# Second half's state-space output moved beside the first half's delta stages, its projection into the expert stage; expert up rows stacked and summed in strips

## What is computed

```python
# end of the first block
y = rms_norm(y * silu(z_ssm), ssm_norm_g)                # (512, 2048)
y_ssm = y @ w_branch_ssm                                 # 2048 x 1024
merged = sigmoid(g_att) * y_att + sigmoid(g_ssm) * y_ssm
x = x + gate * (merged @ w_out)
# second block
h = modulate(rms_norm_2(x, norm1_gain), shift1, scale1)
qa, ka, va, qkv_b, z_b, b_raw, a_raw = split(h @ w_in)   # 512+512+512+1536+512+4+4 columns
x = x + gate1 * (concat(band_attention(qa, ka, va), delta_rule(qkv_b, z_b, b_raw, a_raw)) @ w_out)
h2 = modulate(rms_norm_2(x, norm2_gain), shift2, scale2)
# PEER: per token 8 heads x 16 experts out of 16384
u, vv = expert_down[experts], expert_up[experts]         # rows of 1024
act = gelu(einsum("thkd,td->thk", u, h2))
y = einsum("thk,thkd->td", gates * act, vv)
x = x + gate2 * y
```

## Time and profile before

| | |
|---|---|
| median of 3 runs | 2975.04 us |
| span of the profiled execution | 2961.7 us |
| TensorE busy | 2601.6 us (88%) |
| VectorE busy | 1694.0 us (57%) |
| GpSimd busy | 1163.5 us (39%) |
| ScalarE busy | 790.8 us (27%) |
| DMA, mean over the span | 239 GB/s |
| DMA, expert rows | 147456 packets, 536.94 MB |
| mean granted TensorE clock | 0.954 |

### The profile page before, as it was taken

The page is one execution under the profiler, slowest core; times in us unless marked ns, Lnnn a source line. Parts: engine busy times, 40 slices in busy tenths (PEclk is TensorE's granted clock), DMA queues, the critical chain, the costliest instruction groups (busy, mean ns, idle before and its releaser), DMA issues.

```text
span 2961.7 us, 25890 instructions
## 1 busy us (share of the span) xinstructions
PE 2601.6 (88%) x8302; PEld 1362.8 (46%) x8302; DVE 1694.0 (57%) x3696; ACT 790.8 (27%) x1604; POOL 1163.5 (39%) x1091
## 2 busy tenths in 40 slices
PE   7999899999979979988899899979887777777787
PEld 3444444445544436477775465546432222222232
DVE  2059814345521244274379998765777777777764
ACT  2022402148720022233234323221312221222121
POOL 0000000023300000000057777666777777777776
PEclk8999999999989999999899899989999899999999
DMA  7214112222323233322379989999999999999998
GB/s 310 75 57 171 58 66 79 85 65 69 96 85 119 108 114 118 127 83 75 114 259 355 349 304 379 383 364 343 370 407 405 398 407 404 407 397 409 408 404 351
DMA packets 185462, 709.00 MB, mean 239 GB/s; under 512 B 20416, under 2 KB 43344, under 8 KB 175216
## 3 DMA queue, kind: packets, MB, share of 16 engines
q0 software_dynamic: 147456, 536.94, 47.0%
q1 hardware_dynamic: 37584, 169.45, 15.4%
q10 hardware_dynamic: 288, 0.96, 0.1%
HBM read 703.01 MB, written 4.27 MB: 239 GB/s over the span
## 4 chain that ended last, share of the span: by engine, by line
PE 18%; POOL 17%; issue 8%; DMA 4%; DVE 3%; ACT 0%; POOLq 0%; SPq 0%; DVEq 0%; ACTq 0%
POOL ring L3032 13%; PE bank L3224 11%; PE bank L491 4%; POOL second_arena L3032 4%; DMA ring<-in_peer_expert_down,experts 2%; DVE ring L3107 1%; DMA second_arena<-in_peer_expert_down,experts 1%; DMA x_rows_scratch<-second_arena 0%; DVE second_arena L3107 0%; PE bank L2360 0%; PE bank L2367 0%; PE bank L2365 0%; DMA out<-xT 0%; DMA ring<-in_peer_expert_up,experts 0%; PE bank L2908 0%
## 5 line engine op out<-in xcount | busy, mean ns | idle before, releaser
L3224 PE MATMUL bank<-ring,xT 128*128 128x512 f32 x1516 | 759.3, 638 | 181.4 <-ACT xT L3200 79.9
L3107 DVE CUSTOM_DVE_ANT_0 ring<-ring,second_arena 128x1024 f32<-128x1024 f32 x380 | 465.9, 1226 | 214.7 <-DMA ring<-in_peer_expert_down,experts 171.9
L3224 PEld LDWEIGHTS bank<-ring,xT 128*128 128x128 f32 x1516 | 289.9, 202 | 589.5 <-issue 372.7
L3032 POOL DMA_INDIRECT ring<-in_peer_expert_up,experts x384 | 403.3, 1050 | 154.0 <-issue 97.5
L3032 POOL DMA_INDIRECT ring<-in_peer_expert_down,experts x380 | 401.7, 1057 | 131.5 <-issue 114.3
L491 PE MATMUL bank<-hT,ring 128*128 128x512 f32 (+2 forms) x1168 | 429.8, 527 | 4.6 <-PEq L3337 1.8
L491 PEld LDWEIGHTS bank<-hT,ring 128*128 128x128 f32 (+1 forms) x1168 | 220.8, 191 | 206.8 <-issue 197.4
L3032 POOL DMA_INDIRECT second_arena<-in_peer_expert_down,experts x132 | 141.1, 1069 | 434.3 <-DVE experts L3090 389.9
L1412 POOL TENSOR_TENSOR xs_skip<-xs_rows,rows 128x512 f32<-128x512 f32 x16 | 24.7, 1541 | 708.0 <-ACT xs_rows L1290 618.8
L3200 ACT ACTIVATE xT<-consts,expert_coefs 128x128 f32<-128x128 f32 x505 | 177.9, 395 | 405.2 <-PE bank L3224 273.7
L3224 PE MATMUL bank<-second_arena,xT 128*128 128x512 f32 x504 | 238.8, 605 | 24.5 <-DMA second_arena<-in_peer_expert_up,experts 24.5
(11 more groups left out here) (529 smaller groups left out, 3118.6 us busy)
## 6 DMA issues: line engine op xcount, KB each, us to landing
ring<-in_weights SPq DMA_DIRECT2D x65, 2048.0 KB, 8.1
second_arena<-in_weights SPq DMA_DIRECT2D x12, 1024.0 KB, 8.4
decay<-acum_scratch SPq DMA_DIRECT2D x16, 512.0 KB, 5.3
ring<-in_peer_expert_up,experts POOLq DMA_INDIRECT x384, 6.5
ring<-in_peer_expert_down,experts POOLq DMA_INDIRECT x380, 6.5
second_arena<-in_peer_expert_down,experts POOLq DMA_INDIRECT x132, 6.5
x_rows<-in_x SPq DMA_DIRECT2D x1, 2048.0 KB, 12.0
x_rows_scratch<-second_arena SPq DMA_DIRECT2D x2, 1024.0 KB, 8.7
```

The lines of the kernel that those rows point to most:

```text
L3032: pool.indirect_dma_start(out=slot[seat[n]], out_offset=None, in_=d[f"peer_expert_{kind}_2"], in_offset=bass.IndirectOffsetOnAxis(ap=exper ...
L3107: post(dve, dve.tensor_tensor_reduce(row, row, h_row(i), 1.0, 0.0, ALU.mult, ALU.add, dots[:, u % 2, s:s + 1]), dotted)
L3224: last = pe.matmul(k.bank[half][:], diag[n % DR], row[:, half * 512:(half + 1) * 512], start=(h == 0 and s == 0), stop=(h == RH - 1 and s ...
```

## The change

The change has four parts.

1. **State-space output in halves.** `ssm_out_stage` and `norm_stage` work on the first 256 tokens only. The second half's inputs, `xbcT` (2 MB) and `merged` (1 MB), are written to DRAM at the start of `ssm_out_stage`. `late_ssm_out_stage` (70 + 2 ticks) reads them back and does the second half's gate, branch and output matmuls, with the 8 weight chunks loaded a second time. Behind it stand the second half's norm (`norm3_stage`, 11 ticks) and its gates (`second_gates_stage`, now for one half, 8 ticks). This line stands where the second half's projection stood: beside the first half's band and delta stages. `second_gates_stage` beside the first projection does the first half.
2. **Second half's projection in the expert stage.** `half_projection_stage` of the second half (44 + 10 ticks) stands in `late` behind the first half's queries. Its 7 chunks come as 14 transfers of 1024 KB through two slots that are cut out of the ring's last query slot. That slot's four seats are therefore given to the experts only from job 160 on, not from job 28.
3. **20 ticks to a unit.** `beat(u, s) = (16 u + s) * 5 // 4` takes the place of `16 u + s`.
4. **Up rows stacked, summed in strips.** ScalarE copies each unit's expert numbers (16 copies of 32x4, `stack_experts`) so that one up gather brings, on each block of 32 partitions, one of four experts for the same 32 tokens. The coefficients are copied in the same way (`stack_coefs`, 16 more copies, between `weigh` and the diagonals). The diagonal is 128x32 (`ident32`), 16 buffers of it. Four up gathers make a quad; for each half of the columns four matmuls of 128x32 by 128x512 write the four strips of 32 partitions of a bank. The seats of a quad's four rows come free together. `sum_apart` is gone: TensorE sums all rows of the last unit.

```diff
 def ssm_out_stage(k, t):
-        plan = columns(find(k, "w_in", GS0, 1024), k.hT)
+        first = slice(0, H2)
+        plan = columns(find(k, "w_in", GS0, 1024), k.hT[:, :, first])
...
-        pj = Projection(k, ctx, "ssm_out", plan, banks=range(7))
+        pj = Projection(k, ctx, "ssm_out", plan, banks=range(7), width=H2)
...
+            sp.dma_start(k.kept_y, t.xbcT[:, 0:16, H2:T]).then_inc(kept, 16)
+            sp.dma_start(k.kept_merged, k.merged[:, :, H2:T]).then_inc(kept, 16)
             k.stream(sp, k.modulation.later[-1])
+            sp.wait_ge(kept, 32)
...
 def second_block(k):
...
             beside(k, now, delta=[band_setup_stage(k, t, first, now), band_stage(k, t, first, now), delta_setup_stage(k, t, first, now),
                                   delta_solve_stage(k, t, first, now), delta_scan_stage(k, t, first, now)],
-                   projection=[half_projection_stage(k, t, second, now, ring, list(range(len(chunks))), load, 76)])
+                   late_output=[late_ssm_out_stage(k, t, second, now, ring, lambda sp: ring.stream(sp, len(again) - 1), 70),
+                                norm3_stage(k, t, second, now, "norm2b", "norm1_gain_2", 0, hT, cut(t.arena, 3072, KD, H2), k.bank[6:8]),
+                                second_gates_stage(k, t, second, now, ring, len(again) - 1, k.bank[6:8], 5120,
+                                                   lambda sp: k.stream(sp, n_out, 2))])
...
+        late_in = SmallRing(k, ctx, "late_projection_weights", chunks, [spare[:, 0:4, :], spare[:, 4:8, :]], 2)
...
         late = [early_query_stage(k, t, first, ctx, columns(query_chunks, first.mixT), load_queries),
+                half_projection_stage(k, t, second, ctx, late_in, [(g, g + 1) for g in range(0, len(late_in.chunks), 2)],
+                                      lambda sp: late_in.stream(sp, len(late_in.chunks) - 1), 44),
                 band_stage(k, t, second, ctx), delta_setup_stage(k, t, second, ctx), delta_solve_stage(k, t, second, ctx),
...
 def expert_stage(k, t, halves, late, query_chunks, late_in):
...
-        diag = [spent[:, n // 2, (n % 2) * P:(n % 2 + 1) * P] for n in range(DR)]
+        diag = [spent[:, n // 8, (n % 8) * STRIP:(n % 8 + 1) * STRIP] for n in range(DR)]
+        coef_stacked = [spent[:, 2, RK * n:RK * (n + 1)] for n in range(2)]
...
-        few, some = [list(range(8)), 16], [list(range(8, 12)) + list(range(8)), 28]
+        few, some = [list(range(8)), 16], [list(range(8, 12)) + list(range(8)), 160]
...
+            def stack_coefs(u):
+                act.wait_ge(weighed.sem, u + 1)
+                if u >= 2:
+                    act.wait_ge(diag_ok.sem, (u - 1) * RK)
+                for x in range(4):
+                    for q in range(4):
+                        mine = coef_stacked[u % 2][blocks(x), :].rearrange("p (g q) -> p g q", q=4)[:, :, q]
+                        ins = act.activation(mine, coef[blocks(q), u % 2, 4 * x:4 * x + 4], ACT.Copy)
+                post(act, ins, coef_moved)
...
-                    row = arrived(pe, ("up", u, s))
-                    pe.wait_ge(diag_ok.sem, n + 1)
+                    rows = [arrived(pe, ("up", u, 4 * g + q)) for q in range(4)]
+                    pe.wait_ge(diag_ok.sem, u * RK + 4 * g + 4)
                     for half in range(2):
-                        last = pe.matmul(k.bank[half][:], diag[n % DR], row[:, half * 512:(half + 1) * 512],
-                                         start=(h == 0 and s == 0), stop=(h == RH - 1 and s == RK - 1))
+                        for q in range(4):
+                            last = pe.matmul(k.bank[half][blocks(q), :], diag[(u * RK + 4 * g + q) % DR],
+                                             rows[q][:, half * 512:(half + 1) * 512],
+                                             start=(h == 0 and g == 0), stop=(h == RH - 1 and g == QUADS - 1))
                     last.then_inc(summed, 1)
+                other.upto(beat(u + 2, 0) + 1)
```

393 lines of the change are left out of this document (257 added, 136 removed).

## The result

The changed kernel takes **2956.92 us** (median of 20 runs), the kernel before 2972.1 us beside it (20 runs). The ratio is 0.994, with a 95% interval of 0.9925 to 0.9955: faster by 15 us, where I had forecast 82. The time lies outside my range of 2840 to 2945.

What follows compares the result with a forecast made beforehand. TensorE was taken to bound the state-space output and delta stages, GpSimd's issue and bytes the steady part, mixed engines the late part. Terms -108 - 12 + 22 + 17 - 1 = -82 us gave 2893 us, range 2840 to 2945.

Steps and rivals of the forecast that it cites:

- Step 1: State-space output stage on half the tokens: TensorE's matmuls take half the time, -108 us (-110 to -95).
- Step 2: Norm and gates before the first projection at half width: together -12 us (-9 to -14).
- Step 3: First half's delta stages: TensorE's work exchanged one for one, 97.3 us out, 119.3 in, +22 us.
- Step 4: Late part of the expert stage: strips free TensorE, added weights and denser VectorE work spend it, +17 us (-38 to +84).
- The projection's 54 ticks: Second half's projection in the expert stage: 2.7 units moving 60 MB at 405 GB/s, 148 us.
- Nine units at 51 us on the mean: Other late work, 180 ticks in the expert stage: 459 us, between 404 by bytes and 526 from above.
- The 12 seats, at 0 us: Expert gathers with 12 seats up to job 160: 0 to 16 us, put at 0 because bytes bind there.
- Step 5: Steady part of the expert stage: GpSimd's issue stays, quads and copies are covered, -1 us.
- that rival: Expert stage: less TensorE activity lowers the granted clock to a mean of 0.8, +27 us, 2920 us; chance 12%.
- That strips might not run side by side: Expert stage up rows: strips reading four different rows keep 27.7 us a unit, about +60, 2953 us; chance 3%.
- Only bytes bind: Late expert units: with TensorE free the nine units take 404 us, 2838 us in all; chance 15%.
- The late chain does not compress: Late expert units: handing over between engines sets the length, +122 in place of +17, 2998 us; chance 5%.

Runs made afterwards that it cites:

- seats back early: The changed kernel with its full 16 seats from the 112th gather on instead of the 160th: 2949.89 us, ratio 0.9936 to the kernel before.
- the diagonals: The changed kernel with ScalarE writing a quad's four diagonals in a row before the late work between them: ratio 0.9872 to the kernel before, slower chip.
- strips alone: The kernel before with only the stacked up rows, strips and quads added, 16 ticks a unit: ratios 0.9955 and 0.9958 to the kernel before, slower chips.
- single rows: The changed kernel with stacking and strips undone, up rows summed one at a time, the rest kept: ratios 0.9987 and 0.9989 to the kernel before, slower chips.
- fillers: The changed kernel with three matmuls of zeros behind each quad from unit 3 on: ratio 1.0041 to the kernel before, slower chip.

## Why the prediction was wrong

**Step 1 (state-space output, -108) was right:** 119.8 us for 228.3, TensorE 118.3 of it. **Step 2** was nearly so: -9 with the first loads, for -12.

**Step 3 (delta stages, +22) was 9 us too small.** TensorE's idle time stayed what it was (15.1 us before by the earlier trace rows, 15.5 now), so the exchange of work one for one was the right model. Its records grew by 30.3 us instead of 22. I had priced all at full clock, and the clock fell at the end, where the line's work had run out (0.74 in the last 45 us):

```profile
1282.65 1.94 PE L2596 MATMUL bank<-second_arena 128*64 128x128 f32 x8 [4.29 <-DVE second_arena L2615]
...
1297.62 5.73 PE L1786 MATMUL bank<-hT,ring 128*4 128x256 f32 x32
1303.28 1.09 PE L2596 MATMUL bank<-second_arena 128*64 128x128 f32 x8
```

The scan's eight records take 1.94 us behind an idle 4.3 us and 1.09 after the gates; the eight such groups from 1282 to 1297 us lost some 0.9 us each, and the gates' 5.7 us stand for my 4.2. The mean clock of these stages went from 0.97 to 0.92. That the line's last tick lies inside the scan was right for order and wrong for cover: the scan is a chain, and needs other matmuls between its own.

**Step 4 (late part, +17) is the one that failed**, by 47 us. Its terms:

*The projection's 54 ticks, 2.7 units, at 148 us.* The units took 62.8 + 62.3 + 0.7 x 58.7 = 166 us. I had counted bytes alone and left out where TensorE's 97 us of projection stand (55.4 + 41.9 in step 3). The row chunks cost twice as much per tick, and three of the four stood in one unit, which TensorE then filled. With the shares even the same stretch is 50.9 + 62.2 + 0.7 x 52.6 = 150 us. This error is shown.

*Nine units at 51 us on the mean and 12 us for the rest, 471 us.* It was 500. I had given each unit the price of its fullest engine. Of the eight whole ones seven took 52 to 63 us. In two of them the bytes bind (54.6 and 52.5 us, at 408 and 399 GB/s) and in one TensorE has 53 of 58 us. In the other four no engine is full, as in the one of 62.9 us, in which VectorE has 55 and GpSimd stood in wait for seats for 12; this is the sign of being wrong that I had named, over 56 us with no engine full. GpSimd waited 5 to 17 us for seats in each of the four, 49 us in all; which work held the rows' sums back there was not isolated. Of the 29 us, seats back early return at most 7 and the stacking copies some 10, each by one or two profiles and near what profiles of one kernel differ by. The rest, some 12 us, I can't assign: it goes with neither the clock nor the diagonals, and the number of ticks in a unit is worth some 6 us at most. Nor is it shown that these shares add up: seats returned early and even shares together gave 24 us in the profiles, where apart they gave 7 and 20.

*The 12 seats, at 0 us.* I had bounds of 0 to 16 and took the lower one. In the kernel before they cost 14 us (7 to 22), and the seat waiting that they add is nearly all in the first five late units. What they cost in the change was not run.

**Step 5 was right** on the first chip. The steady part took 795.8 us for 794.0, at a clock of 0.62 for 0.93; quads and copies are covered, as argued. On the slower chips the strips shorten it, which I had not seen.

**The rivals.** The clock came out at 0.82 in the late part, about where that rival had it (0.8), and at 0.62 in the steady part, and no cost of it shows in the expert stage: strips alone at 0.77 need no more time than single rows at 0.95. The Trainium skill, "TensorE: Matmul & The Clock Gate", section "What's actually happening", says that activity releases the throttle. The trace agrees: TensorE's records went from 77% of the steady part to 34% and the clock with them, and fillers brought it up. What doesn't follow from that rule is a longer kernel. That strips might not run side by side fell too: 16 records in 1.92 us. "Only bytes bind" holds in single units (54.6 us at 408 GB/s) and not on the whole. "The late chain does not compress" was nearest: I gave it 60 us as the point from which it decides against the change, and three units of the first nine lie above 62. The cause I gave it, pieces of late work before a quad in which TensorE waits in order, fits the first unit, where a full TensorE fits as well; its size, 122 us, was too large.

## What to carry to other kernels

When work is woven in by ticks, price the ticks, not the stage: a share that costs twice as much in one stretch lengthens that stretch, however much room the mean leaves. A stretch in which three engines are each 60 to 75% busy and share a few buffers took longer here than its fullest engine's time (666 us for 500); before adding work there, look at how long buffers are held against the turn in which they come round, and don't price fewer of them at nothing. And a unit with TensorE freed is worth only what the next limit gives: here 20 us a unit of TensorE were freed, and by the two runs with single rows 29 us in twelve units came of it in the late part.

## What the runs showed of the chip

The lower clock was free in the memory-bound part: 795.8 us at 0.62, 794.0 at 0.93, and on a slower chip 875.0 at 0.59, 876.8 at 0.79. In the delta scan, a chain, it was not: 1.94 for 1.09 us.

A gather's issue on GpSimd is still 0.94 us clear of a dot and up to 1.77 us beside one, as in the earlier trace rows:

```profile
1539.56 0.94 POOL L3171 DMA_INDIRECT ring<-in_peer_expert_down,experts  x1 [0.30 <-issue]
1540.80 1.77 POOL L3171 DMA_INDIRECT ring<-in_peer_expert_up,experts_stacked  x1 [0.30 <-issue]
```

I had not expected chips to differ by so much for one kernel: 2970 and 3086 us for the kernel before, nearly all of it in the gathers of the expert stage (steady part 794 and 891 us). The change seems worth more on the slower ones: 55 us between the two profiled spans there (3078.4 and 3023.0), against 14.5 on the first. One execution each is behind that. In the profiles the kernel before has 17 us more of late part there than on the first chip and the change 2; another 15 us is the steady part (891.3 and 875.9 us), in which the kernel before waits 38 us for seats and the change 0.6. Why seats come free later there is open.
